# One TensorE run less in each pair of a chunked recurrence: own-token products joined to the one-token level

## The chip, the cores and the metric

The kernel runs on one core of one Trainium2 chip. The metric is the device time of one execution in microseconds (us).

## The reference

The program is a chain of three transformer layers on one sequence of 512 tokens, 1024 wide, all in float32. Only the first mixer matters here, an HGRN2 recurrence with 8 heads of 128 by 128:

```python
forget = lb + (1.0 - lb) * sigmoid(f);  key = 1.0 - forget;  log_f = log(forget)
query = silu(q);  value = i
def chunk_step(state, inp):
    qc, kc, vc, gc = inp
    b = jnp.cumsum(gc, axis=2)
    o_inter = jnp.einsum('bhck,bhkv->bhcv', qc * jnp.exp(b), state)
    diff = b[:, :, :, None, :] - b[:, :, None, :, :]
    decay = jnp.exp(jnp.where(causal, diff, -jnp.inf))
    scores = jnp.einsum('bhtk,bhsk,bhtsk->bhts', qc, kc, decay)
    o_intra = jnp.einsum('bhts,bhsv->bhtv', scores, vc)
    ...
o = rmsnorm(o, out_gain) * silu(g)
return o @ w_out
```

Before it lie a norm and the projection to q, f, i, g. After it come the output projection, a SwiGLU layer, a dilated attention layer with its SwiGLU, and a third layer with a gated recurrence.

## The kernel before, in words

Nearly all the time goes to projections. Weights come in panels of 128 by 2048; ScalarE rounds a panel to float32r (`conv`, w_hi), GpSimd makes the rest (w_lo, `lo_piece` in this stage), and TensorE makes three products of 512 columns for each 128 by 128 tile: high by high, high by low, low by high.

The stage of this change works off the 8 heads in 4 pairs, p = 0 to 3 (the first to the fourth). For each pair, scores between tokens of one chunk of 128 are made by levels. Step l = 0 makes each token's product with itself. Step l = 1 joins single tokens to pairs, l = 2 pairs to fours, up to l = 7 (halves of 64). After each of the levels 1 to 7 the queries of later halves (q_dec, `fold_queries` on VectorE) and the keys of earlier halves (`fold_keys` on GpSimd) are multiplied by the decay of the level, and the next level reads both. VectorE moves the scores out of the PSUM banks with a predicated copy (`take_products` for l = 0, `take_level` for the rest). Levels alternate between banks 6 and 5; the products take parts of both.

Each engine's order is written out by hand. TensorE does not stand still while VectorE and GpSimd fold: `LEVEL_SLICES` says how many slices of a projection panel (6 matmuls of 512 columns) follow each level; before there are 8 intervals of them in a pair. In pair p it also works on the two heads of the pair before, in four steps a head (`tail`): 0 keys turned by token, 1 states of the chunks, 2 outputs, 3 the mean square of the norm for heads 5 and later. A head with an earlier number has its mean square made later, where `late_head` says. On VectorE the same head needs `chunk_states`, `head_taken` (the output times gain and gate) and `head_normed` (times the root, then split in high and low: three instructions). ScalarE squares the output (`head_squares`) and makes the root.

What frees what: `lev_free` counts what VectorE has taken; the products of a pair wait for all 16 steps of the pair before, its level 7 included. `mean_squares(hd)` waits until `head_normed(hd - 1)` is done (`oh_ready`), since both use bank 4. `queries(p + 1)` on ScalarE, and before it the `conv` of a panel, wait for whole panels (`panel_done`), and `head_squares` of the pair's second head stands behind both in ScalarE's order.

Of the kernel before, what the change touches and what calls it, by code (L numbers as in the profile page):

```python
# [16 lines left out]
P = 128  # L17
# [5 lines left out]
TT = S // P  # L23
# [7 lines left out]
CUT = 32  # L31
LEVELS = (64, 32, 16, 8, 4, 2, 1)
# [80 lines left out]


SPLIT_HEADS = 5
LEVEL_SLICES = ((3,) * 8, (3,) * 8, (3, 3, 2, 3, 2, 3, 2, 2), (2, 2, 3, 3, 2, 2, 1, 1))
SLICES_BEFORE = [0] + list(itertools.accumulate(n for row in LEVEL_SLICES for n in row))


# [47 lines left out]
def build(nc, wall, x_t, p_t, vecs_d, ident_d, cs_d, lmask_d, amask_d, sel_d, out_t):  # L167
    with ExitStack() as ctx:
# [292 lines left out]

        def late_head(p, l):

            if l == 4 and p:
                return 2 * p - 2
            if l == 0 and p > 1:
                return 2 * p - 3

        def tail_bank(hd):
# [154 lines left out]
        def _(pool):  # L624
# [81 lines left out]
            for p in range(PAIRS):  # L706
                lo_piece(6 + 3 * p, 0, 4) if p == 0 else lo_piece(6 + 3 * p, 2, 4)
                if p < PAIRS - 1:
                    lo_piece(7 + 3 * p, 0, 2)
                    fold_keys(p, 1)  # L710
                    lo_piece(7 + 3 * p, 2, 4)
                    fold_keys(p, 2)
                    fold_keys(p, 3)
                    if p:
                        head_lower(2 * p - 2)
                    lo_piece(8 + 3 * p, 0, 2)
                    fold_keys(p, 4)
                    lo_piece(8 + 3 * p, 2, 4)
                    fold_keys(p, 5)
                    decays(p + 1)  # L720
                    fold_keys(p, 6)
                    lo_piece(9 + 3 * p, 0, 2)
                    if p:
                        head_lower(2 * p - 1)
                    fold_keys(p, 7)
                else:
                    for l in range(1, STEPS):
                        fold_keys(p, l)
                        if l == 3:
                            head_lower(2 * p - 2)  # L730
                        if l in (3, 4):
                            out_pieces(HOUT, 2 * l - 6, 2 * l - 4)
                        elif l == 6:
                            out_pieces(HOUT + 1, 0, 1)
# [14 lines left out]
        def _(act):  # L749
# [196 lines left out]
            def tail(hd, step):  # L946

                if step == 0:
                    keys_by_token(hd)
                elif step == 2:  # L950
                    head_squares(hd)
                elif step == 3 and hd >= SPLIT_HEADS:
                    root_log(hd)
# [5 lines left out]
            for p in range(PAIRS):  # L959
                if 0 < p < PAIRS - 1:  # L960
                    conv(7 + 3 * p)
                for l in range(STEPS):
                    if p == PAIRS - 1 and l in (2, 5):
                        conv(HOUT + l // 3)
                    if p:
                        tail(2 * p - 2 + l // 4, l % 4)
                        late = late_head(p, l)
                        if late is not None:
                            root_log(late)
                            root_exp(late)  # L970
                        if l == (1 if p < PAIRS - 1 else 2):
                            gates(p - 1)
                        if p == PAIRS - 1 and l == 6:
                            gates(p)
                    if p < PAIRS - 1 and l == 2:
                        conv(8 + 3 * p)
                        sigmoids(p + 1)
                    if p < PAIRS - 1 and l == 5:
                        conv(9 + 3 * p)
                        queries(p + 1)  # L980
# [289 lines left out]
        def _(dve):  # L1270
# [169 lines left out]
                dve.wait_ge(panel_done, n + 1)  # L1440
                both_scaled(n, gate[:, 2 * p % 4:2 * p % 4 + 2, :].rearrange("p c s -> p (c s)"), gin_ready, p)

            def take_products(p, a):

                n = 2 * STEPS * p + a
                dve.wait_ge(lev_done, n + 1)
                bank = PB[5 + a][:].rearrange("p (n c) -> p n c", c=P)
                s3 = scores[(2 * p + a) % 4][:].rearrange("p (n c) -> p n c", c=P)
                own = lmask[:, len(LEVELS):len(LEVELS) + 1, :].to_broadcast([P, TT, P])
                nc.vector.copy_predicated(s3, own, bank).then_inc(lev_free, 1)  # L1450

            def take_level(p, l):

# [47 lines left out]
                dve.wait_ge(ohi_made, hd - (HG - 2) + 1)  # L1501
                tt(o_lo[:, hd, :], root_bank(hd)[:], o_hi[:, hd, :].bitcast(F32), ALU.subtract).then_inc(oh_ready, 1)

            def tail(p, hd, step):

                if step == 1:
                    chunk_states(hd)
                elif step == (2 if p < PAIRS - 1 else 3):
                    head_taken(hd)

            forget_in(0)
# [26 lines left out]

            ch.settle()
            for p in range(PAIRS):  # L1540
                for l in range(STEPS):
                    if l == 0:
                        take_products(p, 0)
                        take_products(p, 1)
                    else:
                        fold_queries(p, l)
                        take_level(p, l)
                    if p:
                        tail(p, 2 * p - 2 + l // 4, l % 4)
                        if l == (1 if p < PAIRS - 1 else 2):  # L1550
                            gate_in(p - 1)
                        if p == PAIRS - 1 and l == 6:
                            gate_in(p)
                    if l == 5 and p:
                        head_normed(2 * p - 2)
                    if l == 1 and p > 1:
                        head_normed(2 * p - 3)
                    if p < PAIRS - 1:
                        if l == 2:
                            forget_in(p + 1)  # L1560
                        elif l == 3:
                            forgets(p + 1)
                        elif l == 5:
                            keys(p + 1)
                            query_in(p + 1)
                        elif l == 7:
                            first_decay(p + 1)
            chunk_states(HG - 2)
            chunk_states(HG - 1)
            head_normed(HG - 3)  # L1570
# [311 lines left out]
        def _(pe):  # L1882
# [180 lines left out]
            def near(t, n):  # L2063
                return t[:, n * P:(n + 1) * P]
# [42 lines left out]
            def level(p, l, a):  # L2107

                n = 2 * STEPS * p + 2 * l + a
                q = query if l == 0 else q_dec[p % 2]  # L2110
                if a == 0 and l == 0:
                    pe.wait_ge(query_ready, p + 1)
                    pe.wait_ge(key_ready, p + 1)
                elif a == 0:
                    pe.wait_ge(qdec_ready, STEPS * p + l)
                    if l > 1:
                        pe.wait_ge(kend_ready, (STEPS - 1) * p + l - 1)
                if a == 0:
                    if l == 0 and p or l == 1:
                        pe.wait_ge(lev_free, 2 * STEPS * p + 2 * l)  # L2120
                    elif l > 2:
                        pe.wait_ge(lev_free, 2 * STEPS * p + 2 * l - 2)
                for c in range(TT * a, TT * a + TT):
                    if l == 0:
                        for b in range(P // CUT):
                            at = slice(CUT * b, CUT * (b + 1))
                            ins = mm(near(PB[5 + a], c - TT * a)[at, at], near(key[p % 2], c)[:, at], near(q, c)[:, at])
                    elif span_of(l) >= LEAST_BLOCK:
                        for b in range(P // (2 * span_of(l))):
                            ins = early_late(near(level_bank(l), c // 2), near(key[p % 2], c), near(q, c),  # L2130
                                             span_of(l), b, (c % 2) * P // 2)
                    else:
                        for b in range(P // CUT):
                            at, to = slice(CUT * b, CUT * (b + 1)), c * P // 2 + b * CUT // 2
                            ins = mm(level_bank(l)[at, to:to + CUT // 2], near(key[p % 2], c)[:, at],
                                     halves_of(near(q, c)[:, at], l)[1])
                ins.then_inc(lev_done, 1)
# [61 lines left out]
            for p in range(PAIRS):  # L2199
                for l in range(STEPS):  # L2200
                    level(p, l, 0)
                    level(p, l, 1)
                    if p:
                        tail(2 * p - 2 + l // 4, l % 4)
                        late = late_head(p, l)
                        if late is not None:
                            mean_squares(late)
                    done = SLICES_BEFORE[STEPS * p + l]
                    for n in range(done, done + LEVEL_SLICES[p][l]):
                        panel_slice(6 + n // KC, n % KC)  # L2210
# [318 lines left out]
```

## Time and profile before

| what | value |
|---|---|
| median of 3 runs | 2110.53 us (2109.53 to 2110.65) |
| the profiled execution | 2110.24 us, of it 2108.4 us span |
| TensorE busy | 2097.6 us (99% of the span) |
| GpSimd, VectorE, ScalarE busy | 1144.4, 1006.3, 746.2 us |
| granted TensorE clock, mean | 0.999 |
| the four pairs of the recurrence | 74.57 to 236.96 us of the span |

The span is the profiled time from the first to the last instruction; 1.8 us of the execution lie outside it. TensorE is the engine to watch: the others have idle time.

### The profile page before, as it was taken

To read this page: it belongs to the slowest core of one execution; us is meant where nothing else is said; L and a number is where in the kernel's file an instruction comes from. 1 tells how busy PE (TensorE), PEld (TensorE's weight loads), DVE (VectorE), ACT (ScalarE), POOL (GpSimd) and SP (SyncE) were. 2 spreads that over 40 slices of the span, in tenths; PEclk is the share of its full clock that TensorE was granted. 3 is DMA by queue.
4 is the path that set the end of the run, shared out by engine and by line. 5 is a ranking of instruction groups with operands and counts; after the bars stand their busy time and mean duration, and the time that the engine had idled before them with its cause. 6 is when DMAs were issued, how large, how long until landed. Compare 5 with 4: busy or idle time off the path is not lost.

```text
span 2108.4 us, 28021 instructions
## 1 busy us (share of the span) xinstructions
PE 2097.6 (99%) x11130; PEld 1743.4 (83%) x11130; DVE 1006.3 (48%) x1144; ACT 746.2 (35%) x867; POOL 1144.4 (54%) x821
## 2 busy tenths in 40 slices
PE   9999999999999999999999999999999999999998
PEld 7888888888888889888888888888888888888887
DVE  6256555554123265634544333733477544553226
ACT  6335542222224455533222233514443332222234
POOL 6677465555555343375555555544566455555553
PEclk9999999999999999999999999999999999999999
DMA  5212132222232212132222222222222222223321
GB/s 193 86 62 82 41 114 88 97 99 100 100 107 102 100 62 99 60 120 100 99 99 99 100 100 100 100 99 100 85 96 99 100 100 99 97 87 107 118 100 61
DMA packets 32441, 203.34 MB, mean 96 GB/s; under 512 B 3432, under 2 KB 6248, under 8 KB 8688
## 3 DMA queue, kind: packets, MB, share of 16 engines
q1 hardware_dynamic: 32224, 202.21, 27.9%
q8 instruction: 54, 0.88, 0.2%
q14 instruction: 19, 0.16, 0.0%
q10 hardware_dynamic: 144, 0.09, 0.0%
HBM read 200.19 MB, written 2.10 MB: 96 GB/s over the span
## 4 chain that ended last, share of the span: by engine, by line
PE 96%; DVE 2%; ACT 1%; DMA 0%; issue 0%; POOL 0%; SPq 0%; DVEq 0%; ACTq 0%
PE bank L1884 96%; DVE x L1767 0%; DMA h<-x_t 0%; PE bank L2252 0%; DVE sgate L1816 0%; DVE aqk L1590 0%; ACT w_hi L753 0%; PE bank L2146 0%; DVE h L1817 0%; POOL first_wlo L697 0%; DVE ssq L1841 0%; DVE bank L1587 0%; PE bank L2273 0%; DVE rot L1588 0%; ACT sgate L753 0%
## 5 line engine op out<-in xcount | busy, mean ns | idle before, releaser
L630 POOL TENSOR_TENSOR w_lo<-raw,w_hi 128x512 fp32r<-128x512 f32 x676 | 977.5, 1476 | 863.9 <-ACT w_hi L753 863.9
L1884 PE MATMUL bank<-u_hi,w_hi 128*128 128x512 f32 (+1 forms) x1936 | 753.5, 390 | 0.1
L1884 PE MATMUL bank<-u_lo,w_hi 128*128 128x512 f32 (+1 forms) x1936 | 749.4, 387 | 0.0
L753 ACT ACTIVATE w_hi<-raw 128x2048 fp32r<-128x2048 f32 x185 | 354.3, 1915 | 923.2 <-PE bank L1884 921.7
L1884 PE MATMUL bank<-u_hi,w_lo 128*128 128x512 f32 (+1 forms) x1936 | 482.1, 387 | 0.0
L1884 PEld LDWEIGHTS bank<-u_hi,w_hi 128*128 128x128 f32 x1936 | 363.6, 188 | 74.5 <-ACTq L1160 0.5
L1884 PEld LDWEIGHTS bank<-u_lo,w_hi 128*128 128x128 f32 x1936 | 363.7, 188 | 73.7 <-issue 0.2
L1884 PEld LDWEIGHTS bank<-u_hi,w_lo 128*128 128x128 f32 x1936 | 362.5, 188 | 74.6
L1884 PE MATMUL bank<-act_hi,w_hi 128*128 128x512 f32 x528 | 205.4, 389 | 0.0
L1884 PE MATMUL bank<-act_lo,w_hi 128*128 128x512 f32 x528 | 205.4, 389 | 0.0
L1299 DVE TENSOR_TENSOR h<-h,bank 128x512 f32<-128x512 f32 x48 | 30.8, 684 | 300.3 <-PE bank L1884 300.3
L1327 DVE TENSOR_TENSOR sq<-bank,rstd 128x512 f32<-128x512 f32 x66 | 45.7, 692 | 262.7 <-PE bank L1884 236.8
L1884 PE MATMUL bank<-act_hi,w_lo 128*128 128x512 f32 x528 | 125.5, 389 | 0.0
L1331 DVE TENSOR_TENSOR un<-un,sq 128x512 f32<-128x512 f32 x66 | 88.2, 1337 | 75.7 <-ACT sq L753 75.7
L1884 PEld LDWEIGHTS bank<-act_lo,w_hi 128*128 128x128 f32 x528 | 99.1, 188 | 20.6
L1884 PEld LDWEIGHTS bank<-act_hi,w_lo 128*128 128x128 f32 x528 | 99.1, 188 | 20.6
L1884 PEld LDWEIGHTS bank<-act_hi,w_hi 128*128 128x128 f32 x528 | 99.1, 188 | 20.5
L1333 DVE TENSOR_TENSOR act_lo<-un,act_hi 128x512 f32 x66 | 101.0, 1531 | 8.1
L753 ACT ACTIVATE u_hi<-h,vecs 128x512 fp32r<-128x512 f32 x56 | 37.5, 716 | 150.1 <-DVE h L1299 146.4
L649 POOL TENSOR_TENSOR w_lo<-raw,w_hi 128x512 fp32r<-128x512 f32 x56 | 76.3, 1388 | 22.2 <-ACT w_hi L753 22.0
L1290 DVE TENSOR_TENSOR ssq<-ssq,sq 128x512 f32<-128x512 f32 x49 | 73.7, 1504 | 29.1 <-ACT sq L753 25.8
L1332 DVE CAST act_hi<-un 128x512 f32 x66 | 82.3, 1247 | 9.7 <-DVE un L1331 3.7
(286 smaller groups left out, 2119.7 us busy)
## 6 DMA issues: line engine op xcount, KB each, us to landing
raw<-wall SPq DMA_DIRECT2D x185, 1024.0 KB, 4.9
out_t<-h SPq DMA_DIRECT2D x8, 256.0 KB, 2.5
h<-x_t SPq DMA_DIRECT2D x3, 512.0 KB, 6.5
first_raw<-wall SPq DMA_DIRECT2D x6, 256.0 KB, 6.8
h<-x_t SPq DMA_DIRECT2D x2, 256.0 KB, 4.2
first_raw<-wall SPq DMA_DIRECT2D x4, 128.0 KB, 4.4
lmask_f<-lmask_in SPq DMA_DIRECT2D x1, 512.0 KB
cs<-cs_in SPq DMA_DIRECT2D x1, 512.0 KB, 3.5
```

The lines of the kernel that those rows point to most:

```text
L630: ins = nc.gpsimd.tensor_tensor(w_lo[:, s, c], raw[:, s, c], w_hi[:, s, c].bitcast(F32), ALU.subtract)
L649: ins = nc.gpsimd.tensor_tensor(w_lo[:, s, c], raw[:, s, c], w_hi[:, s, c].bitcast(F32), ALU.subtract)
L753: return nc.scalar.activation(out, in_, func, **k)
L1290: ins = tt(total[:], total[:], sq[:, n % 2, :], ALU.add)
L1299: tt(h[:, j, :], h[:, j, :], pair(g0 + q)[c][:], ALU.add).then_inc(h_ready, 1)
L1327: tt(sq[:, s, :], pair(g)[0][:], rstd[:], ALU.mult).then_inc(sgin_ready, 1)
L1331: ch.link(tt(un[:, s, :], un[:, s, :], sq[:, s, :], ALU.mult))
L1332: ch.link(cp(act_hi[:, i * 2 + s, :], un[:, s, :]))
L1333: tt(act_lo[:, i * 2 + s, :], un[:, s, :], act_hi[:, i * 2 + s, :].bitcast(F32), ALU.subtract).then_inc(act_ready, 1)
L1884: return nc.tensor.matmul(out, lhsT, rhs, start=start, stop=stop, skip_group_check=True)
```

## The change

The products of the tokens with themselves are made in half of bank 5, block by block beside each other, for the whole pair. The one-token level follows them at once. The slices of the pair go into seven intervals; their sums (24, 24, 20, 16) stay. `take_products` reads the compact bank in four strips of 32 partitions. The steps of the two heads of the pair before go into seven intervals as well; some of the work around them moves by one interval, and in the last interval `first_decay` goes between the fold and `take_level`.

```diff
-LEVEL_SLICES = ((3,) * 8, (3,) * 8, (3, 3, 2, 3, 2, 3, 2, 2), (2, 2, 3, 3, 2, 2, 1, 1))
+LEVEL_SLICES = ((0, 4, 4, 4, 3, 3, 3, 3), (0, 4, 4, 4, 3, 3, 3, 3), (0, 4, 3, 3, 3, 3, 2, 2), (0, 4, 2, 3, 2, 2, 2, 1))
+HEAD_STEPS = {1: ((0, 0),), 2: ((0, 1),), 3: ((0, 2),), 4: ((0, 3), (1, 0)), 5: ((1, 1),), 6: ((1, 2),), 7: ((1, 3),)}
...
         def late_head(p, l):
-            if l == 4 and p:
+            if l == 5 and p:
                 return 2 * p - 2
-            if l == 0 and p > 1:
+            if l == 1 and p > 1:
                 return 2 * p - 3
...
                 if p < PAIRS - 1:
-                    lo_piece(7 + 3 * p, 0, 2)
                     fold_keys(p, 1)
-                    lo_piece(7 + 3 * p, 2, 4)
+                    lo_piece(7 + 3 * p, 0, 4)
                     fold_keys(p, 2)
...
-                for l in range(STEPS):
-                    if p == PAIRS - 1 and l in (2, 5):
-                        conv(HOUT + l // 3)
+                for l in range(1, STEPS):
+                    if p == PAIRS - 1 and l == 2:
+                        conv(HOUT)
                     if p:
-                        tail(2 * p - 2 + l // 4, l % 4)
+                        for e, step in HEAD_STEPS[l]:
+                            tail(2 * p - 2 + e, step)
...
+                        if p == PAIRS - 1 and l == 5:
+                            conv(HOUT + 1)
...
-                    if p < PAIRS - 1 and l == 2:
+                    if p < PAIRS - 1 and l == 3:
                         conv(8 + 3 * p)
                         sigmoids(p + 1)
...
+            def take_products(p):
+                dve.wait_ge(lev_done, 2 * STEPS * p + 2)
+                for b in range(P // CUT):
+                    at = slice(CUT * b, CUT * (b + 1))
+                    bank = PB[5][at, 0:2 * TT * CUT].rearrange("p (n c) -> p n c", c=CUT)
+                    s3 = scores_of_pair[p % 2][at, :].rearrange("p (n c) -> p n c", c=P)[:, :, at]
+                    own = lmask[at, len(LEVELS):len(LEVELS) + 1, at].to_broadcast([CUT, 2 * TT, CUT])
+                    ins = nc.vector.copy_predicated(s3, own, bank)
+                ins.then_inc(lev_free, 2)
...
-                elif step == (2 if p < PAIRS - 1 else 3):
+                elif step == 2:
                     head_taken(hd)
...
-                for l in range(STEPS):
-                    if l == 0:
-                        take_products(p, 0)
-                        take_products(p, 1)
-                    else:
-                        fold_queries(p, l)
-                        take_level(p, l)
+                for l in range(1, STEPS):
+                    fold_queries(p, l)
+                    if l == 1:
+                        take_products(p)
+                    elif l == STEPS - 1 and p < PAIRS - 1:
+                        first_decay(p + 1)
+                    take_level(p, l)
...
-                    if l == 5 and p:
+                    if l == 6 and p:
                         head_normed(2 * p - 2)
-                    if l == 1 and p > 1:
+                    if l == 2 and p > 1:
                         head_normed(2 * p - 3)
                     if p < PAIRS - 1:
-                        if l == 2:
+                        if l == 3:
                             forget_in(p + 1)
-                        elif l == 3:
+                        elif l == 4:
                             forgets(p + 1)
                         elif l == 5:
                             keys(p + 1)
                             query_in(p + 1)
-                        elif l == 7:
-                            first_decay(p + 1)
...
-                    if l == 0 and p or l == 1:
-                        pe.wait_ge(lev_free, 2 * STEPS * p + 2 * l)
-                    elif l > 2:
+                    if l == 0 and p:
+                        pe.wait_ge(lev_free, 2 * STEPS * p)
+                    elif l > 1:
                         pe.wait_ge(lev_free, 2 * STEPS * p + 2 * l - 2)
...
-                            ins = mm(near(PB[5 + a], c - TT * a)[at, at], near(key[p % 2], c)[:, at], near(q, c)[:, at])
+                            ins = mm(PB[5][at, CUT * c:CUT * (c + 1)], near(key[p % 2], c)[:, at], near(q, c)[:, at])
```

## Rows read from the trace of the kernel before

**Rows 1.** The page, part 1: busy us, share, instructions of each engine.

```profile
PE 2097.6 (99%) x11130; PEld 1743.4 (83%) x11130; DVE 1006.3 (48%) x1144; ACT 746.2 (35%) x867; POOL 1144.4 (54%) x821
```

**Rows 2.** Busy by stretch, the third pair: stretch, us, busy, PEclk granted clock.

```profile
160.39:201.00 40.61, 40.61 (x603) 33.08 (x602) 29.45 (x40) 23.71 (x23) 31.21 (x28) 1.00 0.24 80
```

**Rows 3.** TensorE's timeline, first pair: start us, us, instruction, [idle before].

```profile
74.57 0.76 PE L1884 MATMUL bank<-query,key 128*32 128x32 f32 x64
...
79.00 0.39 PE L1884 MATMUL bank<-u_lo,w_hi 128*128 128x512 f32 x1
79.23 0.39 PE L1884 MATMUL bank<-u_hi,w_lo 128*128 128x512 f32 x1
79.55 0.74 PE L1884 MATMUL bank<-q_dec,key 128*32 128x16 f32 x64
80.21 0.50 PE L1884 MATMUL bank<-u_hi,w_hi 128*128 128x512 f32 x1
80.55 0.39 PE L1884 MATMUL bank<-u_lo,w_hi 128*128 128x512 f32 x1
```

**Rows 4.** One line's instructions, TensorE's small matmuls: ns least/median/most.

```profile
L1884 PE MATMUL bank<-q_dec,key x1472: 176/183/270, 79.5 to 234.5; 128*32 128x16 f32 x128, 128*16 128x16 f32 x32, 128*32 128x32 f32 x16, 128*64 128x64 f32 x8
```

**Rows 5.** Lines of VectorE's predicated copy of the products, and its shortest copy.

```profile
L1450 DVE COPY_PREDICATED score_pair<-lmask,bank x8: 720/736/751, 75.2 to 202.2; 128x512 f32<-128x512 uint8 x8
L1468 DVE COPY ssq<-bank x7: 273/301/319, 122.6 to 239.9; 128x128 f32<-128x128 f32 x7
```

**Rows 6.** TensorE's timeline, end of the third pair: levels 6 and 7, next products.

```profile
191.86 0.70 PE L1884 MATMUL bank<-q_dec,key 128*32 128x32 f32 x32
...
196.99 1.15 PE L1884 MATMUL bank<-q_dec,key 128*64 128x64 f32 x16
...
201.01 0.76 PE L1884 MATMUL bank<-query,key 128*32 128x32 f32 x64
```

**Rows 7.** ScalarE's timeline there: panel, queries, the second head's square.

```profile
192.03 1.91 ACT L753 ACTIVATE w_hi<-raw 128x2048 fp32r<-128x2048 f32 x1 [4.45 <-PE bank L1884]
...
196.22 0.58 ACT L753 ACTIVATE sq<-bank 128x512 f32<-128x512 f32 x1
```

**Rows 8.** VectorE's timeline there: head_normed, head_taken, fold, take_level, first_decay.

```profile
189.57 0.69 DVE L1488 TENSOR_TENSOR bank<-bank,gate 128x512 f32<-128x512 f32 x1
...
191.03 0.69 DVE L1490 TENSOR_TENSOR o_lo<-bank,o_hi 128x512 fp32r<-128x512 f32 x1
...
196.83 0.75 DVE L1481 SCALAR_TENSOR_TENSOR gate<-bank,vecs,gate 128x512 f32<-128x512 f32 x1 [0.98 <-ACT sq L753]
198.18 1.19 DVE L1435 TENSOR_TENSOR q_dec<-q_dec,decay 128x512 f32<-128x512 f32 x1 [0.59 <-PE bank L1884]
199.28 0.73 DVE L1458 COPY_PREDICATED score_pair<-lmask,bank 128x512 f32<-128x512 uint8 x1
199.91 1.44 DVE L1426 TENSOR_TENSOR q_dec<-query,forget 128x1024 f32<-128x1024 f32 x1
```

**Rows 9.** GpSimd's timeline there.

```profile
197.54 1.27 POOL L688 TENSOR_TENSOR sum_lo<-sq,sum_hi 128x512 fp32r<-128x512 f32 x1
198.77 1.50 POOL L683 TENSOR_TENSOR key<-key,decay 128x512 f32<-128x512 f32 x1
200.23 3.52 POOL L649 TENSOR_TENSOR w_lo<-raw,w_hi 128x512 fp32r<-128x512 f32 x2
```

**Rows 10.** TensorE's timeline, end of the fourth pair: levels 6, 7, head 5's mean square.

```profile
229.77 0.70 PE L1884 MATMUL bank<-q_dec,key 128*32 128x32 f32 x32
...
233.54 1.15 PE L1884 MATMUL bank<-q_dec,key 128*64 128x64 f32 x16
234.61 1.12 PE L1884 MATMUL bank<-sq,ones_r 128*128 128x512 f32 x2
```

**Rows 11.** ScalarE's timeline there: the square of head 5.

```profile
232.26 0.60 ACT L753 ACTIVATE sq<-bank 128x512 f32<-128x512 f32 x1 [3.57 <-PE bank L1884]
```

**Rows 12.** VectorE's timeline there: the gate of the fourth pair.

```profile
232.71 1.27 DVE L1386 TENSOR_TENSOR gate<-bank,rstd 128x512 f32<-128x512 f32 x2
```

More of the change, by code:

```diff
@@ L1441, in gate_in @@
                 both_scaled(n, gate[:, 2 * p % 4:2 * p % 4 + 2, :].rearrange("p c s -> p (c s)"), gin_ready, p)
[L1443 to L1450, printed above, removed]
+            def take_products(p):
[7 more added lines that the diff above has]
+                ins.then_inc(lev_free, 2)
             def take_level(p, l):
@@ L1502, in last_lower, with tail @@
                 tt(o_lo[:, hd, :], root_bank(hd)[:], o_hi[:, hd, :].bitcast(F32), ALU.subtract).then_inc(oh_ready, 1)
-            def tail(p, hd, step):
+            def tail(hd, step):
                 if step == 1:
                     chunk_states(hd)
-                elif step == (2 if p < PAIRS - 1 else 3):
+                elif step == 2:
                     head_taken(hd)
@@ L1540, in _ @@
             for p in range(PAIRS):
-                for l in range(STEPS):
-                    if l == 0:
-                        take_products(p, 0)
-                        take_products(p, 1)
-                    else:
-                        fold_queries(p, l)
-                        take_level(p, l)
+                for l in range(1, STEPS):
[5 more added lines that the diff above has]
+                    take_level(p, l)
                     if p:
-                        tail(p, 2 * p - 2 + l // 4, l % 4)
+                        for e, step in HEAD_STEPS[l]:
+                            tail(2 * p - 2 + e, step)
                         if l == (1 if p < PAIRS - 1 else 2):
@@ L2202, in _ @@
                     level(p, l, 1)
-                    if p:
-                        tail(2 * p - 2 + l // 4, l % 4)
+                    if p and l:
+                        for e, step in HEAD_STEPS[l]:
+                            tail(2 * p - 2 + e, step)
                         late = late_head(p, l)
```

## The prediction

> **What bounds the kernel now.** I read the page first: TensorE is busy 99% of the span [rows 1], and its chain of waits holds nothing else to speak of. So a change of the order is worth what it takes from or adds to TensorE's time, and nothing on any other engine counts until TensorE waits for it. Then I read the busy time by stretch over the recurrence: in the third pair TensorE is busy 40.61 of 40.61 us at a granted clock of 1.00 (of 2.4 GHz) while GpSimd has 31.21 and VectorE 29.45 [rows 2]. The other pairs are the same in this: TensorE never waits in the stage. The reader is to see two things: there is no stall to remove, so that the gain can only be in the small cost of changing between kinds of matmul; and GpSimd and VectorE, at 77% and 73% of the third pair, have little room there. So the third view is TensorE's timeline around one level [rows 3], and the fourth the timelines of all engines at the ends of the pairs [rows 6 to 12], where I laid the new order over the old durations.
>
> **What the merge saves.** In a panel, matmuls of 512 columns start 0.23 us apart (79.00, 79.23). The first small matmul of a level starts 0.32 us after the last large one (79.23 to 79.55): 0.09 lost. After the level, the second large one starts 0.34 after the first (80.21, 80.55): 0.11 lost [rows 3]. Inside the 0.66 us from the level's first matmul to the first large one there is also the time that the last small matmul takes to run out; the rows don't part it off. It is between nothing and the length of one, 0.18 us [rows 4]; I take the middle, 0.1. A run that joins the one before it pays each of these once less: 0.30 us, between 0.20 and 0.38. It happens once in each of 4 pairs: 4 x 0.30 = 1.2 us saved (0.8 to 1.5). The matmuls themselves stay: 32 tiles' worth of 32 columns for the products of a pair (64 in the trace, two passes each), as many for the level, and 84 slices in all. The steps of the heads still hang on a level each, so they save and cost nothing.
>
> **What is added on VectorE, and its cover.** `take_products` was two copies of 0.736 us [rows 5] and is now four, each on 32 partitions with half of the columns. No row shows that form. Bounds for one are the shortest copy of a bank, 0.3, and the old form's 0.74 [rows 5]: 1.2 to 2.9 us for four against 1.47. Half the columns put it between, at 0.5: 2.0 us. They stand behind `fold_queries(p, 1)`, and `take_level(p, 1)` behind them. TensorE needs them at level 2 only, which starts after the run and 4 slices of 6 x 0.23 = 1.37 us: at least 5.5 us later. A fold of 0.6 and 2.9 of copies end before that. Cost: nothing. Without the slices it would be the whole 2.6 us.
>
> The lost wait of level 1 for the products gives nothing, as no wait shows there. GpSimd's order changes in one place: `fold_keys(p, 1)` ahead of two pieces of the panel. The fold, 1.5 to 2 us, and four pieces, 1.27 us each when nothing is in their way [rows 9], then end 7 to 8 us after level 1, about 1 us after level 2 is done; `fold_keys(p, 2)` follows (under 2 us), and level 3 starts at least 5 us after level 2 is done. Cost nothing, with 2 us of room at the least. SP's queue is untouched in order: a load is let go by `lo_ready` and starts with the pieces, up to 2 us sooner, no later.
>
> **Where the order makes TensorE wait: end of the third pair.** I count from the start of the level 6 run (191.86). Both orders have done 16 slices of the pair by then, so panel 13 is complete and ScalarE begins the next panel's conversion at +0.17 (192.03), then the queries, then the square of head 3 at +4.36 (196.22) [rows 6, 7]. VectorE's `head_taken(3)` starts when this lands, at +4.97 (196.83), and lasts 0.75: +5.72 [rows 8]. Up to here nothing moves. Behind it stood the fold of level 7. Now `head_normed(2)` stands between, moved from interval 5 to 6: three instructions, 189.57 to 191.72, 2.15 us [rows 8]: +7.87; the next starts about 0.1 before an instruction ends: +7.8. Level 7's scores are there from +6.32 (198.18, when the fold was let go) [rows 8], so the fold is now 1.5 us late. After it (0.6 us, 1.19 with GpSimd in its way) comes `first_decay(3)`, which was behind `take_level` and is ahead now: 1.44. Then `take_level(2, 7)`, 0.73. Sum: 7.8 + 0.6 + 1.4 + 0.7 = +10.5. TensorE is at the products of the fourth pair at 201.01, +9.15 [rows 6], both intervals with 2 slices as before, and they wait for this `take_level`. Stall: 1.4 us.
>
> GpSimd adds to it. The fold at 198.18 took 1.19 us and ended 0.6 after the GpSimd instruction of 197.54 had ended (198.81) [rows 8, 9]: it had stood until that was over. In the new order a piece of w_lo (1.27 us or more) can be in front of `first_decay` in the same way. So the stall is 1.4 to 2.7; I take 2.0. The Trainium skill, "SBUF — State Buffer", section "SBUF: two separate sides", says that a VectorE instruction with two SBUF inputs and a GpSimd instruction take an exclusive lock in turn, and the loser waits for the whole of the other; by that rule, the trace agrees, the stall would be the 2.7, and the total 0.7 above mine.
>
> What is queued behind the waiting TensorE is only itself; the wait moves the fourth pair as a whole. The same order at the end of the second pair has 3 slices in each interval: `head_normed(0)` ends there before level 7's scores come, and fold, `first_decay` and `take_level` (2.8 to 4) fit in what TensorE has to do from that point to the next pair: 201.01 - 196.99 with 2 slices, 1.37 more with 3, less the 1.19 until the scores are there, 4.2 us [rows 6, 8]. In the first pair there is no head at all. Cost there nothing, with the room small.
>
> **The second wait: end of the fourth pair.** I count from the level 6 run, 229.77. In the new order its interval has 2 slices where it had 1: level 7 starts at 3.77 + 1.37 = +5.14, and `mean_squares(5)` 1.07 behind it (233.54 to 234.61) [rows 10], at +6.2. It waits for `head_normed(4)`, which before was done in interval 5 and now stands in interval 6 behind `head_taken(5)` and `gate_in(3)`. The square of head 5 starts at +2.49 (232.26) and lasts 0.60 [rows 11]; `head_taken(5)` 3.1 to 3.85; the gate 1.27 [rows 12] and its own completion, 0.26, to +5.35; the three instructions 2.15: +7.5. Stall: 1.3 us (1.0 to 1.6, by the small gaps between these). The last fold and `take_level` then end before the turned keys need them, since TensorE has the mean square and a slice ahead of that.
>
> **Sum.** -1.2 + 2.0 + 1.3 = +2.1 us. The profiled execution, 2110.24 with 2108.4 of span, would become 2112.3; it stands 0.3 under the median of the runs, 2110.53, which becomes 2112.6. A measurement of this kernel tells about 0.2%, 4.2 us, from no change. So I forecast: same, with the sign of a small loss.
>
> **Rivals.**
> A. The merge works and no wait comes: -1.2, 2109.3. For it: TensorE has no wait in the whole stage now. Against it: both waits come out of durations in the rows, one with 1.4 us, one with 1.3 to spare for errors. Chance 0.2.
> B. Only one of the two waits comes: +0.1 to +0.8, about 2111. For it: a stall of TensorE shifts all that is behind it, and ScalarE may be earlier. Chance 0.17.
> C. Forecast, both waits: +1.3 to +3.2, 2111.8 to 2113.7. Chance 0.54.
> D. Slower by more than 4.2 us: the waits bring TensorE's clock down to its lower level, 1.2 GHz, for some time after each. At half clock a 512-column matmul would start each 0.46 instead of 0.23 us, so each microsecond of work costs one more. With +2.1 already there, it decides from 2.1 us of work at half clock on, one short spell behind either wait. Against it: the clock stands at 1.00 in the stretch [rows 2], and no row here shows it fall after a wait as short. The Trainium skill, "TensorE: Matmul & The Clock Gate", Part 1, says that the clock gate halves the clock after idleness; no run here shows it, and by it this rival would be the outcome if a stall were long enough. Chance 0.05.
> E. The merge is worth more than the rows say and the waits hide in it: it would need 4.2 us, over 1 us a pair, where the whole run of products has 0.76 us [rows 3]. Chance of faster by over 0.2%: 0.03. The last 0.01 is for a slower outcome from something unseen.
>
> **How the numbers follow.** The likeliest is C with 2112.6. The range takes in A at its middle (2109.3, and 0.3 for the spread of runs) and B, and goes above C to both waits at their upper bounds, 2110.5 - 0.8 + 2.7 + 1.6 = 2114.0 and 0.5 for spread: 2109.0 to 2114.5. It leaves out D and E and a part of A. Faster 0.03, slower 0.06, same 0.91.
>
> **What the profile after would show.** In each pair, the products and the level stand in one TensorE run of about 1.3 us with no large matmul between, and the first two pairs take 0.3 us less each. TensorE's timeline has an idle of 1.4 to 2.7 us before the fourth pair's products, released by VectorE's `take_level`, and one of about 1.3 before the mean square of head 5, released by `head_normed`. `take_products` is four copies of about 0.5 us with no wait behind them. The prediction is wrong if one of the idles is missing, if a level 2 or 3 run waits for the products or for GpSimd, or if the granted clock leaves 1.00.

## The result: slower by 0.26%, outside of the forecast's range

| | median | lowest to highest | runs |
|---|---|---|---|
| before | 2109.53 us | 2108.97 to 2110.65 | 9 |
| changed | 2115.45 us | 2112.30 to 2117.42 | 9 |

The ratio is 1.0026, 95% interval 1.0017 to 1.0035. The median moved by +5.9 us, where +2.1 was forecast, and the executions now lie 5 us apart where they lay within 2. The profiled execution of the changed kernel, 2113.23 us, is the second shortest of its nine: what it shows is less than what the median lost.

The page of the changed kernel, part 1, against [rows 1]:

```profile
PE 2096.8 (99%) x11130; PEld 1744.3 (83%) x11130; DVE 1005.8 (48%) x1152; ACT 745.8 (35%) x867; POOL 1143.8 (54%) x821
```

The work is the same, so the loss is idle time or clock. The chain of waits puts names to it; this view lists what TensorE waited for, in us, times, longest:

```profile
PE bank L1888 <- DVE score_pair L1463: 2.3, 1, 2.3
PE bank L1888 <- DVE o_lo L1495: 1.2, 1, 1.2
```

These are the two waits of the forecast: `take_level` of the third pair's level 7 (L1463), and `head_normed` (L1495). Now the timeline of VectorE in front of the first, which answers to [rows 8]:

```profile
195.05 0.75 DVE L1486 SCALAR_TENSOR_TENSOR gate<-bank,vecs,gate 128x512 f32<-128x512 f32 x1 [1.74 <-ACT sq L753]
195.72 0.69 DVE L1493 TENSOR_TENSOR bank<-bank,gate 128x512 f32<-128x512 f32 x1
196.44 0.69 DVE L1494 CAST o_hi<-bank 128x512 fp32r<-128x512 f32 x1
197.17 0.69 DVE L1495 TENSOR_TENSOR o_lo<-bank,o_hi 128x512 fp32r<-128x512 f32 x1
197.78 0.82 DVE L1438 TENSOR_TENSOR q_dec<-q_dec,decay 128x512 f32<-128x512 f32 x1
198.52 2.29 DVE L1429 TENSOR_TENSOR q_dec<-query,forget 128x1024 f32<-128x1024 f32 x1
200.73 0.72 DVE L1463 COPY_PREDICATED score_pair<-lmask,bank 128x512 f32<-128x512 uint8 x1
```

From `head_taken` on nothing has a gap: this is one chain of VectorE to the end of `take_level` at 201.45, and TensorE starts the products at 201.60. `first_decay` took 2.29 us where it took 1.44. GpSimd had begun its pieces of w_lo 0.5 us before it, the first of them took 1.72 us, and the second began only at 199.69; in the kernel before, the pieces began behind `first_decay` (200.23 against 199.91 [rows 8, 9]):

```profile
198.00 3.94 POOL L650 TENSOR_TENSOR w_lo<-raw,w_hi 128x512 fp32r<-128x512 f32 x2
```

TensorE's timeline, the merged run of the first pair and the two waits:

```profile
73.60 0.75 PE L1888 MATMUL bank<-query,key 128*32 128x32 f32 x63
74.16 0.20 PE L1888 MATMUL bank<-q_dec,key 128*32 128x16 f32 x1
...
74.86 0.50 PE L1888 MATMUL bank<-u_hi,w_hi 128*128 128x512 f32 x1
...
201.60 0.89 PE L1888 MATMUL bank<-query,key 128*32 128x32 f32 x62 [2.29 <-DVE score_pair L1463]
...
203.85 0.78 PE L1888 MATMUL bank<-sum_hi,ones_r 128*128 128x512 f32 x1
204.42 0.63 PE L1888 MATMUL bank<-sum_lo,ones_r 128*128 128x512 f32 x1
...
237.64 1.13 PE L1888 MATMUL bank<-sq,ones_r 128*128 128x512 f32 x2 [1.23 <-DVE o_lo L1495]
```

The run of products and level takes 1.26 us to the first large matmul. But behind the first wait the matmuls of 512 columns take 0.78 and 0.63 us instead of the 0.48 and 0.40 elsewhere. The busy time by stretch tells why; each line gives the stretch, its length, the busy time of TensorE, its weight loads, VectorE, ScalarE and GpSimd, then the granted clock, the DMA share and GB/s:

```profile
201.00:202.00 1.00, 0.40 (x43) 0.43 (x47) 0.45 (x1) 0.00 (x0) 0.94 (x1) 0.96 0.00 0
202.00:203.00 1.00, 1.00 (x93) 1.00 (x87) 0.00 (x0) 0.00 (x0) 0.00 (x0) 0.50 0.00 0
...
204.00:205.00 1.00, 1.00 (x4) 0.81 (x4) 0.97 (x4) 0.75 (x2) 1.00 (x1) 0.50 0.87 360
205.00:206.00 1.00, 1.00 (x5) 0.77 (x4) 0.85 (x3) 1.00 (x1) 0.46 (x1) 0.84 1.02 434
206.00:207.00 1.00, 1.00 (x6) 0.81 (x5) 1.00 (x1) 0.97 (x3) 0.00 (x0) 1.00 0.30 115
```

After 2.29 us of idleness TensorE ran from about 202 to 205.3 at its lower level, 1.2 GHz. Before, this stage stood at 1.00 throughout [rows 2]. I take the stage as the time from the first pair's products to the first turned keys of the last heads: 162.39 us before, 166.39 in this execution. The waits are 3.52 of it and the merge gives 1.2 back; about 1.7 us are left for the clock. A start that was 1 us shorter in this execution (73.60 against 74.57) hides some of it in the span, 2111.4 against 2108.4.

### The profile page after: what moved, and what is told of

Read it like the earlier page. It is cut to its first block, busy times and chain, and to the rows that moved or that the text cites. A ratio compares the mean times of both kernels' runs of the same rounds, so it can differ in the third digit from the quotient of the medians.

```text
span 2111.4 us, 28024 instructions
## 1 busy us (share of the span) xinstructions
PE 2096.8 (99%) x11130; PEld 1744.3 (83%) x11130; DVE 1005.8 (48%) x1152; ACT 745.8 (35%) x867; POOL 1143.8 (54%) x821
## 4 chain that ended last, share of the span: by engine, by line
PE 96%; DVE 2%; ACT 1%; issue 0%; DMA 0%; SPq 0%; DVEq 0%; ACTq 0%
PE bank L1888 95%; DMA first_raw<-wall 0%; DVE x L1771 0%; PE bank L2257 0%; DVE sgate L1820 0%; ACT w_hi L753 0%; DVE aqk L1594 0%; PE bank L2150 0%; DVE h L1821 0%; DVE ssq L1845 0%; DVE bank L1591 0%; PE bank L2278 0%; DVE rot L1592 0%; ACT sq L753 0%; ACT sgate L753 0%
```

## The experiments

Two theories at first. Theory 1: waits, less the merge, plus the lower clock behind a wait. Theory 2: something else than waits and clock, in the merged run or elsewhere. A third loss showed up on the way. Each number is a median of 11 executions (6 in changed_again), beside the kernel before on the same chip. The experiments ran on three chips; the medians of the kernel before on them lie between 2109.35 and 2109.74.

**waits_filled.** The two waits stay, and TensorE multiplies ones by ones in them.

```diff
                     if l == 0 and p:
+                        if p == PAIRS - 1:
+                            pe.wait_ge(lev_free, 2 * STEPS * p - 2)
+                            for n in range(10):
+                                mm(near(PB[5], n % TT), ones[:], ones[:])
                         pe.wait_ge(lev_free, 2 * STEPS * p)
...
             def mean_squares(hd):
+                if hd == SPLIT_HEADS:
+                    pe.wait_ge(lev_free, 2 * STEPS * PAIRS - 2)
+                    for n in range(5):
+                        mm(near(PB[5], n % TT), ones[:], ones[:])
```

> The changed kernel, with matmuls of ones by ones put into TensorE's two waits: 10 before the products of the fourth pair, 5 before the mean square of head 5; they write a bank that is free there and is written anew afterwards. The waits stay as long as they are, but TensorE is not idle in them. Theory 1 (the waits of 2.3 and 1.2 us cost 3.5 us, less 1.2 us for the merge, and the rest of the measured +5.9 us is TensorE's clock at its lower level for some us behind a wait): the granted clock is 1.00 at every place, and the time is +2 to +3 us over the kernel before, 2111.5 to 2112.5, with a spread between executions as small as before's (under 2 us). Theory 2 (the clock is a side effect, and what is over 2.3 us comes from another place, the small matmuls or the later stages): it stays near +5.9 us, 2115.4.

Measured: 2111.76 us (2111.43 to 2113.12), before 2109.51: +2.25, ratio 1.0012 (1.0003 to 1.0021). The timeline shows the fill where the wait was, and the stretch with it stands at clock 1.00:

```profile
199.23 2.40 PE L1888 MATMUL bank<-ones_r 128*128 128x128 f32 x20
201.59 0.75 PE L1888 MATMUL bank<-query,key 128*32 128x32 f32 x63
```

```profile
197.00:215.00 18.00, 18.00 (x340) 1.00 0.18 60
```

The products start at the same point (201.59 against 201.60), so the wait is as long as it was; yet 3.7 us of the changed kernel's 5.9 are gone, and so is the spread. That is what theory 1 expected. It is not a clean test of the clock alone, and theory 2 is not out: the 10 matmuls also move the code behind them, which mattered, as later runs show. No run here fills the waits and leaves the code where it was.

**both_back.** Both causes taken back, the merged run kept.

```diff
         def late_head(p, l):
-            if l == 5 and p:
+            if l == 4 and p:
                 return 2 * p - 2
...
-                    elif l == STEPS - 1 and p < PAIRS - 1:
-                        first_decay(p + 1)
                     take_level(p, l)
+                    if l == STEPS - 1 and p < PAIRS - 1:
+                        first_decay(p + 1)
...
-                    if l == 6 and p:
+                    if l == 5 and p:
                         head_normed(2 * p - 2)
```

> The changed kernel with both causes taken back: the first head's late mean square in interval 4 and its head_normed in interval 5, as in the kernel before, and first_decay behind take_level. The merged run and the seven intervals stay. Theory 1: no wait on TensorE in the stage, clock 1.00, and -1.2 us against before (0.8 to 1.5), 2108.3. Theory 2 (the loss is in the merged run or in the four strips): it stays slower than before by 2 us or more.

Measured: 2109.55 us (2107.89 to 2110.70), before 2109.51. TensorE waits for no engine in the stage, which takes 161.21 us against 162.39, 1.18 less, as this stretch shows:

```profile
73.66:234.87 161.21, 161.21 (x2383) 131.28 (x2383) 97.70 (x143) 74.10 (x70) 118.33 (x96) 1.00 0.20 68
```

The merge is worth what was forecast in this execution, but the median doesn't have it. So a third thing takes time in others.

**first_wait_only and second_wait_only.** head_normed and the late mean square taken back in the fourth pair alone, or in the first three alone. The second has `first_decay` behind `take_level` as well, by the same lines as in both_back, which are left out here:

```diff
-            if l == 5 and p:
+            if l == (4 if p == PAIRS - 1 else 5) and p:
...
-                    if l == 6 and p:
+                    if l == (5 if p == PAIRS - 1 else 6) and p:
```

```diff
-            if l == 5 and p:
+            if l == (5 if p == PAIRS - 1 else 4) and p:
...
-                    if l == 6 and p:
+                    if l == (6 if p == PAIRS - 1 else 5) and p:
```

> The changed kernel with head_normed and the late mean square taken back to intervals 5 and 4 in the fourth pair alone: only the wait before the fourth pair's products is left (2.3 us in the profile). Theory 1: +2.3 - 1.2 = +1.1 us, and 1.5 to 3 us more for the clock: +2.5 to +4 us. If the clock loss of the changed kernel comes with the second wait instead, it is +1.1 us with a mean clock of 0.999.

> The changed kernel with head_normed, the late mean square and first_decay taken back in the first three pairs alone: only the wait before head 5's mean square is left (1.2 us in the profile). Theory 1 with the clock falling only behind the long wait: 1.2 - 1.2 = 0 us against before, clock 0.999. If the clock falls behind this wait too in part of the executions: +1 to +3 us with a wide spread.

Measured: first wait alone 2114.33 us (2109.97 to 2116.00), +4.8; second alone 2109.89 (2109.23 to 2112.30), +0.4; before 2109.51. The waits in the profiles are 2.31 and 1.22 us. The kernel with the first wait carries the loss and the spread: +4.8 is more than 2.3 - 1.2 and the 1.5 to 3 us that I gave to the clock. Behind the second the clock stays at 1.00 in the profile:

```profile
215.00:240.00 25.00, 23.78 (x284) 1.00 0.17 49
```

**before_stalled.** The kernel before, and five reductions that nothing reads in front of its `take_level`.

```diff
                         fold_queries(p, l)
+                        if p == 2 and l == STEPS - 1:
+                            for r in range(5):
+                                nc.vector.tensor_reduce(cols[:, r, :], h[:, 0:TT, 0:P], AX_X, ALU.max)
                         take_level(p, l)
```

> The kernel before, with nothing of the change, and one artificial delay: between the fold and take_level of level 7 in the third pair, VectorE reduces 128x512 elements five times into columns that nothing reads, some 0.7 us each. take_level ends 3 us later, and TensorE, which had 1 us of room, should wait some 2.3 us before the fourth pair's products. Theory 1 (a wait of this length is followed by a spell at the lower clock whatever the kernel around it): the clock stands at about 0.5 for 1 to 4 us behind the wait, and the time is +3.5 to +5 us over before with a spread of several us. Theory 2 (the merged run of small matmuls is what the clock falls for): clock 1.00 behind the wait, and +2.3 us.

Measured: 2112.24 us (2111.02 to 2113.88), before 2109.35: +2.9, with a wait of 2.03 us. In the profiled execution, 2111.43 us, the clock stayed at 1.00, and its +2.1 is the wait alone: no trace shows the fall in this kernel. What speaks for it is the mean clock of an execution: it is 0.999 in the six up to 2112.24, and 0.998 in all five from 2112.78 up. That is a coarse sign, since the mean takes in the end of the program, where TensorE has no more work: the profiled execution of both_back has 0.998 too, with the clock at 1.00 in the whole stage and at 0.50 from 2100 us on. The likeliest reading is that the clock falls behind such a wait in part of the executions, with nothing of the change in the kernel; where it fell is not shown. My expectation of +3.5 to +5 was too high for the median.

**decay_behind, both_back_again and changed_again.** The first puts `first_decay` behind `take_level` and changes nothing else; the others are the kernels of both_back and of the change once more.

> The changed kernel with first_decay put back behind take_level, and nothing else. first_decay took 2.29 us in the changed kernel's profile, all of it ahead of take_level, so the first wait should shrink from 2.3 us to 0.3 or less; the second, 1.2 us, stays. Theory 1: 0.3 + 1.2 - 1.2 us, no long wait and so hardly any loss of clock: +0 to +1 us, 2109.5 to 2110.5. If head_normed's place alone were enough for the first wait, it stays over 1 us and the time over +2 us.

> The same kernel as both_back, for a second look: there the stage is 1.2 us shorter in the profile, but the median of the executions stands level with before. If the merge is worth 1.2 us in every execution, the median is 2108.3 and the first was chance; if it is again within 0.5 us of before, something outside of the stage takes 1 us back in most executions, and this execution's profile may show where.

> The changed kernel once more, for the profile of another execution and the spread. Theory 1: again waits of 2.3 and 1.2 us, and a spell at the lower clock behind the first, behind the second, or behind both; the executions over 2115 us must have lost 3 us or more to it.

Measured: decay_behind 2112.59 (2110.74 to 2113.86), both_back_again 2108.44 (2107.79 to 2111.46), changed_again 2116.29 (2115.41 to 2116.93), before 2109.35. The expectation for decay_behind missed by 2 us, and all three profiles show why: an idle that belongs to no engine. TensorE's timeline of both_back_again, then of changed_again:

```profile
199.01 0.75 PE L1888 MATMUL bank<-query,key 128*32 128x32 f32 x63
...
201.85 0.21 PE L1888 MATMUL bank<-q_dec,key 128*32 128x16 f32 x2 [1.52 <-issue]
```

```profile
201.61 0.74 PE L1888 MATMUL bank<-query,key 128*32 128x32 f32 x63 [2.31 <-DVE score_pair L1463]
...
205.53 0.24 PE L1888 MATMUL bank<-q_dec,key 128*32 128x16 f32 x2 [2.61 <-issue]
```

The last 2 of the run's 128 small matmuls start 1.5 and 2.6 us after the others, released by "issue": no semaphore. In both_back_again the only transfer from 198 to 202 was a packet on the instruction queue. The DMA view of 199 to 200, cut in 40 slices (the DMA line) and with the queue's total:

```profile
DMA  0000000090000000000000000000000000000000
...
q8 instruction: 1, 0.02, 7.9%
```

One packet of 16 KB, at 199.2, right behind the run's start at 199.01; TensorE goes on 2.6 us later. In the same view of both_back, from 195.9 to 198, the packet stands 3 us ahead of the products (199.16), and there is no idle:

```profile
DMA  0000009000000000000000000000000000000000
...
q8 instruction: 1, 0.02, 3.8%
```

So theory 3: in the fourth pair the merged run, 64 + 64 matmuls with as many weight loads, is 256 instructions in 1.3 us. Where the code's next piece is asked for only at its start or later, the run is through before the piece has come. The profiles with the merged run and the code up to it in its old place bear it out. In the five with the packet about 3 us or more ahead of the products (the changed kernel's first, waits_filled, both_back, first_wait_only, second_wait_only; it stands between 196.1 and 196.4) the run has no such idle. In the three with a packet within the run it has one: both_back_again as above, changed_again with the packet at 202.6 and work going on 2.9 us later, and decay_behind with the packet at 201.4 and work going on 2.4 us later.

In changed_again all three losses come together: 2.31, 2.61 and 1.22 us of idleness, and the clock at the lower level for nearly 7 us, from 202.9 on, through the second idle and 4 us of work behind it:

```profile
203.00:205.00 2.00, 0.00 (x0) 0.50 0.87 258
205.00:207.00 2.00, 1.48 (x7) 0.50 0.66 274
207.00:209.00 2.00, 2.00 (x7) 0.50 0.00 0
209.00:211.00 2.00, 2.00 (x9) 0.83 0.00 0
```

(In this stretch the columns are us, TensorE's busy time, clock, DMA share, GB/s.) decay_behind had 1.73 us of this idle, the second wait of 1.23, and one more that I had not seen coming: 0.74 us of the level for `first_decay`, since in a merged run the level needs it at once. Putting it behind `take_level` moves the wait from the products to the level:

```profile
201.31 0.72 PE L1888 MATMUL bank<-q_dec,key 128*32 128x16 f32 x62 [0.74 <-DVE q_dec L1429]
203.75 0.21 PE L1888 MATMUL bank<-q_dec,key 128*32 128x16 f32 x2 [1.73 <-issue]
```

**both_back_shifted, slice_between, changed_shifted.** Three tests of theory 3: 64 more instructions ahead of the run (in the third pair's level 4, half done twice), in both_back and in the changed kernel; and one slice inside the fourth pair's run.

```diff
-                for c in range(TT * a, TT * a + TT):
+                for c in list(range(TT * a, TT * a + TT)) * (2 if (p, l, a) == (2, 4, 0) else 1):
```

```diff
-... (0, 4, 2, 3, 2, 2, 2, 1))
+... (1, 3, 2, 3, 2, 2, 2, 1))
```

> both_back, with half of level 4 in the third pair done twice (16 matmuls that write the same scores again: 64 more instructions on TensorE's queue with the weight loads and two passes, 0.3 us of work, no wait and no new change between kinds of matmul). It moves TensorE's code by a quarter of a 16 KB piece. Theory 3 (the third loss: TensorE idles 1.5 to 2.6 us at the end of the fourth pair's merged run in some executions because the next 16 KB of its code, which the instruction queue fetches from the run's first matmul on, isn't there yet; the run is 256 instructions in 1.3 us, exactly such a piece): with the piece's border moved into the run, the fetch begins some us earlier, the idle is gone in every execution, and the median is 2109.5 - 1.2 + 0.3 = 2108.5 with no execution over 2109.5. Rival (the idle is a semaphore or a transfer that the code's place doesn't touch): a spread up to 2110.7 or more, as in both_back.

> both_back, with one of the four slices of the fourth pair's first interval put between the products and the one-token level, so that this pair's run is in two parts again. Theory 3: the same 256 instructions and 24 more now take 2.9 us instead of 1.3, so the idle for code shrinks by 1.4 us or more, from 1.5 to nothing or nearly so, for 0.3 us of a second change of matmul: median 2108.3 to 2108.8, executions over 2109.8 gone. Rival: unchanged spread, and 0.3 us above both_back.

> The changed kernel with the same 64 instructions put in. The waits for VectorE, 2.3 and 1.2 us, stay and are not filled. Theories 1 and 3 together: no idle for code, but still the lower clock behind the first wait: 2109.5 - 1.2 + 0.3 + 3.5 = 2112.1 and 0 to 2.5 us more for the clock, median about 2113.5; the executions of 2115 to 2117 us, which had all three, are gone. If the clock alone made them, the median stays at 2115.5 or above.

Measured, before 2109.44: both_back_shifted 2108.63 (2108.10 to 2109.24), slice_between 2108.62 (2107.88 to 2109.11), changed_shifted 2113.25 (2111.69 to 2114.24). All three came in as theory 3 has it. What the shift and the slice take away from both_back is the spread: 2.8 and 3.7 us in its two sets of executions, 1.1 and 1.2 here. The median says less, as both_back stood at +0.04 and -0.91 us against before, and these two at -0.8. In the profile of both_back_shifted the packets stand at 194.0 and 201.5, ahead of the run and just behind it (199.81 to 201.1). In slice_between the late packet came too, at 198.94, within the slice of this view (198.9 to 199.9) that follows the run's start at 198.85:

```profile
DMA  0900000000000000000000000000000000000000
```

and made no idle, since the level now starts at 201.13 and ends its run 2.9 us behind the packet:

```profile
201.13 0.74 PE L1888 MATMUL bank<-q_dec,key 128*32 128x16 f32 x64
201.82 0.53 PE L2150 MATMUL bank<-ident,key 128*128 128x128 f32 x3
```

The slice has its price: the stage takes 161.52 us (73.36 to 234.88), 0.3 more than in both_back.

In changed_shifted the mean clock is again 0.999 in the five executions up to 2112.48 and 0.998 in the six from 2113.25 up.

**normed_back.** slice_between with `first_decay` ahead of `take_level`, as in the changed kernel.

> slice_between, but with first_decay left ahead of take_level as in the changed kernel: the head's late mean square and head_normed alone are taken back, and one slice stands between products and level in the fourth pair. It tells how much of the first wait was first_decay's place. From the durations: level 7 of the third pair is there 6.3 us after level 6 starts, fold 0.7, first_decay 1.4 to 2.3 (it took 2.29 with GpSimd in its way), take_level 0.7: 9.1 to 10.0, against 9.15 when TensorE comes. Theory 1: a wait of 0 to 0.8 us before the products, no clock loss, median 2108.6 to 2109.4. If head_normed's place was the whole cause, no wait and 2108.6.

Measured: 2110.04 us (2109.30 to 2110.75), before 2109.74; the wait is 1.06 us, 0.3 over my bound, as fold and `first_decay` took 1.18 and 2.07:

```profile
196.82 1.18 DVE L1438 TENSOR_TENSOR q_dec<-q_dec,decay 128x512 f32<-128x512 f32 x1 [0.60 <-PE bank L1888]
197.92 2.07 DVE L1429 TENSOR_TENSOR q_dec<-query,forget 128x1024 f32<-128x1024 f32 x1
199.92 0.72 DVE L1463 COPY_PREDICATED score_pair<-lmask,bank 128x512 f32<-128x512 uint8 x1
```

So each of the two moves makes a wait by itself: `first_decay` ahead of `take_level` 1.06 us here, `head_normed` one interval later 0.74 us in decay_behind, before the level. Neither alone makes the 2.3.

## Why the prediction was wrong

**The merge, -1.2 us.** Right: -1.18 in the stage of both_back. As a whole slice_between is 0.8 us under before, ratio 0.9997 (0.9988 to 1.0006), which is not resolved; nor is both_back_shifted, with the same -0.8.

**The strips of `take_products`, hidden.** Right. They took 0.45 us each where I took 0.5, and nothing waited for them:

```profile
L1454 DVE COPY_PREDICATED score_pair<-lmask,bank x16: 425/446/467, 77.1 to 205.4; 32x256 f32<-32x256 uint8 x16
```

**The first wait, 2.0 us (1.4 to 2.7).** Right in place and cause, 2.29. Counted from the start of level 6 (190.08), `head_taken` ended at +5.72 as worked out and `head_normed` at +7.78 against +7.87; `take_level` ended at +11.37, where the sum had +10.5 without GpSimd. The difference is `first_decay`, which did stand behind a GpSimd piece, as the upper bound had it. **The second, 1.3 us (1.0 to 1.6).** Right, 1.23. **The sum, +2.1.** With the clock kept up and the code's place moved it is +2.25 (waits_filled). The forecast stood on a median of 3 executions, 2110.53; that of the 9 is 2109.53. On the latter the range would have ended 1 us lower, and the measured time came out above it even so.

**What failed is the step from the sum to the time: that nothing else would change with it.** Two mechanisms are missing from the sum, each of them put at nothing.

One was there as rival D, with a chance of 0.05: the clock. I argued from "no row here shows it fall after a wait as short". But no wait of that length was in the trace at all, apart from its end, where TensorE has run out of work. There the clock does leave 1.00: from 2102.0 us to the end of the span, 2108.4, the granted clock before is 0.66, so the trace had a row of the clock falling in idleness. The absence of a row for a short wait was taken for a row. The fall was the common outcome: the mean clock of all but one of the changed kernel's 9 executions was below before's 0.999. By changed_shifted the waits and the clock make +3.8, 0.3 of it extra matmuls; less 2.3 for waits and merge, an estimate of the clock's cost is 1.2 us in the median. Where it falls it costs more: the six executions with the lower mean clock have their middle at 2113.9, the five others at 2112.2, 1.7 us apart. The profile of the changed kernel says the same: about 3.4 us of work at half clock, 1.7 us lost. The Trainium skill, "TensorE: Matmul & The Clock Gate", Part 1, says that the clock stands at half after idleness, and the traces agree in kind: in the four profiles it fell 0.1 to 1.2 us after the 2.3 us of idleness had ended. I held the lack of a row against it.

The other was in none of the rivals: the code's next piece. I counted the merged run as the same matmuls one behind the other and did not ask whether the queue has the instructions at that rate. The difference of the medians without and with the shift, 5.9 (6.9 in changed_again) against 3.5, gives it an estimated 2.4 to 3.4 us in the changed kernel, some of it through a longer spell at the low clock (changed_again). The Trainium skill, "Runtime: NRT & Kernel Launch", section "Instruction fetch mechanics", says that code comes in blocks of 16 KB, 256 instructions, each fetched while the one before it runs, and that this is mostly hidden. The block's size agrees with the packets here; hidden it is not, where 256 instructions pass in 1.3 us and work goes on 2.4 to 2.9 us behind the packet.

**Open.** Why the packet comes 3 us ahead of the run in some executions and within it in others, in the same kernel, no run here tells. In how many executions each of the two losses comes is not measured; only the profiled ones show it. Neither was tried what length of a wait the clock stands: it fell behind 2.3 us in all four profiles with that wait unfilled, not in the one with 2.03, and not behind the waits of 1.0 to 1.2.

## What to carry to other kernels

When TensorE has no wait, an order that makes one costs more than the wait: here a spell at half clock came behind 2.3 us of idleness in all four profiles that have it, so give such a case a chance of its own, and by what the trace contains, not by what it lacks. Where work moves past a hand-over, add up the whole chain on the other engine up to the next point at which TensorE needs it; here that sum named both waits to 0.3 us. A long run of very small matmuls is also a load on the code's supply: a slice of large ones inside it cost 0.3 us here and covered the fetch.

## What the runs showed of the hardware that I had not expected

Where a packet of 16 KB on the instruction queue came within a run of 256 instructions, TensorE stopped for 1.5 to 2.6 us and went on 2.4 to 2.9 us behind the packet. With the code moved by 64 instructions the profile has no such stop, and the spread that went with it is gone. With matmuls of ones on a free bank through both waits the clock stood at 1.00 in the profile (waits_filled). `first_decay`, a VectorE instruction with two inputs of 128x1024, took 1.20 us (before_stalled) to 2.29, with 1.44, 1.68 and 2.07 between; the longest was the one that began 0.5 us behind the start of a GpSimd piece of w_lo.
